# Start-up loads, a head-wise sum moved one step on, and a split output transfer in a two-block transformer kernel on one Trainium2 core

## The reference, cut to what matters

```python
def _rmsnorm(x, g, eps=EPS):
    xf = x.astype(jnp.float32)
    y = xf * lax.rsqrt(jnp.mean(xf * xf, axis=-1, keepdims=True) + eps)
    return (y * g.astype(jnp.float32)).astype(x.dtype)
...
    kk = heads(k * k_k)
    kk = kk / jnp.maximum(jnp.linalg.norm(kk, axis=-1, keepdims=True), 1e-12)
...
    bonus = jnp.sum(rh * kh * r_k.astype(jnp.float32), axis=-1, keepdims=True) * vh
    y = y + bonus.reshape(B, S, RW_WIDTH)
```

## Time and profile before

| | |
|---|---|
| median of three runs | 4110.72 us (4109.21 to 4110.77) |
| the profiled execution's own time | 4109.02 us |
| its span in the profile | 4107.2 us |
| granted TensorE clock, mean | 0.981 |
| TensorE matmul busy | 3915.6 us (95%) |
| VectorE, ScalarE, GpSimd busy | 1750.6, 604.4, 1216.3 us |
| weights read by SyncE's queue | 544.81 MB |

### The profile page before, as it was taken

How to read it: one execution, slowest core, us unless ns; L and a number is a source line. 1 busy time by engine, 2 the same in 40 slices (tenths; PEclk the granted TensorE clock), 3 DMA queues, 4 the chain that set the end, 5 groups by cost and what they waited for, 6 DMA issues and landing times.

```text
span 4107.2 us, 65406 instructions
## 1 busy us (share of the span) xinstructions
PE 3915.6 (95%) x28356; PEld 3601.6 (88%) x28356; DVE 1750.6 (43%) x3176; ACT 604.4 (15%) x1311; POOL 1216.3 (30%) x719
## 2 busy tenths in 40 slices
PE   8999999999999698999999999989998899999997
PEld 7788888888888698999999998877687899999997
DVE  1344425541111443111115447561432588887544
ACT  0333311111111101000000000131302111111001
POOL 0000000001110675777770000000151377775000
PEclk9999999999999898999999999999999999999998
DMA  6555654445543443444444554435332244444441
GB/s 237 188 202 200 219 208 172 168 163 219 191 166 116 152 147 120 165 165 168 176 168 153 170 200 166 160 106 176 66 136 103 105 165 167 175 173 160 164 161 71
DMA packets 105134, 665.69 MB, mean 162 GB/s; under 512 B 21712, under 2 KB 23840, under 8 KB 74384
## 3 DMA queue, kind: packets, MB, share of 16 engines
q1 hardware_dynamic: 61904, 544.81, 36.8%
q0 software_dynamic: 19408, 70.79, 5.4%
q10 hardware_dynamic: 23536, 45.92, 3.1%
HBM read 611.34 MB, written 50.13 MB: 161 GB/s over the span
## 4 chain that ended last, share of the span: by engine, by line
PE 92%; DVE 3%; ACT 2%; issue 1%; DVEq 1%; POOL 0%; ACTq 0%; DMA 0%; POOLq 0%
PE product_bank L538 47%; PE product_bank L586 31%; PE product_bank L382 3%; PE mixer_bank L1214 2%; PE mixer_bank L724 1%; PE mixer_bank L740 1%; PE mixer_bank L2149 1%; ACT xT L841 0%; PE mixer_bank L2150 0%; PE mixer_bank L1234 0%; DVE arena L1328 0%; PE mixer_bank L1104 0%; PE mixer_bank L2181 0%; PE mixer_bank L1086 0%; PE mixer_bank L2114 0%
## 5 line engine op out<-in xcount | busy, mean ns | idle before, releaser
L586 PE MATMUL product_bank<-hT,weight_ring 128*128 128x256 f32 x3648 | 815.6, 382 | 0.0
L586 PEld LDWEIGHTS product_bank<-hT,weight_ring 128*128 128x128 f32 x3648 | 693.9, 191 | 103.5 <-issue 8.3
L538 PE MATMUL product_bank<-hT,weight_ring 128*128 128x128 f32 x3680 | 457.5, 276 | 12.3 <-DVEq L1586 5.8
L538 PEld LDWEIGHTS product_bank<-hT,weight_ring 128*128 128x128 f32 x3680 | 435.9, 193 | 14.6 <-DVEq L1586 6.0
L538 PE MATMUL product_bank<-arena,weight_ring 128*128 128x128 f32 x3232 | 402.4, 275 | 0.0
L538 PEld LDWEIGHTS product_bank<-arena,weight_ring 128*128 128x128 f32 x3232 | 382.2, 192 | 0.6
L562 DVE TENSOR_TENSOR arena<-product_bank,arena 128x128 f32<-128x128 f32 x128 | 37.2, 291 | 744.9 <-PE product_bank L538 743.2
L505 POOL TENSOR_TENSOR arena<-weight_ring 128x1024 f32<-128x1024 f32 x90 | 212.3, 2359 | 420.0 <-PE product_bank L538 295.7
L2549 DVE SCALAR_TENSOR_TENSOR arena<-arena 128x256 f32<-128x256 f32 x176 | 321.9, 1867 | 14.7 <-ACT arena L2514 11.3
L508 POOL TENSOR_TENSOR weight_ring<-weight_ring 128x1024 f32<-128x1024 f32 x112 | 275.3, 2458 | 0.0
L538 PE MATMUL product_bank<-hT,arena 128*128 128x128 f32 x2048 | 250.2, 276 | 1.5 <-DVE hT L494 1.5
(11 more groups left out here) (490 smaller groups left out, 5395.0 us busy)
## 6 DMA issues: line engine op xcount, KB each, us to landing
weight_ring<-in_weights SPq DMA_DIRECT2D x213, 2048.0 KB, 8.1
weight_ring<-in_weights SPq DMA_DIRECT2D x128, 512.0 KB, 5.6
weight_ring<-in_weights SPq DMA_DIRECT2D x64, 384.0 KB, 5.6
units<-out_stage ACTq DMA_DIRECT2D x87, 256.0 KB, 7.9
rwkv_keep<-arena ACTq DMA_DIRECT2D x16, 1282.0 KB, 7.3
arena<-rwkv_keep POOLq DMA_DIRECT2D x8, 2048.0 KB, 9.4
arena<-units POOLq DMA_DIRECT2D x52, 256.0 KB, 3.8
arena<-units POOLq DMA_DIRECT2D x48, 128.0 KB, 6.0
```

Of the source, the lines that this page charges most:

```text
L538: mm = pe.matmul(bank[:, at * P:at * P + P], lhs[:, j, :], rhs[:, j, :], start=g == 0 and n in (0, 3) and j == 0, stop=g == n_groups - 1 a ...
L586: mm = pe.matmul(psg[b][:, half * T:half * T + T], lhs, rhs, start=k == 0, stop=k == 15)
```

## The change

The constants come in two transfers: columns 0 to 383 right behind x, under x's semaphore, which thereby counts to 32, and the rest behind the parameters. ScalarE, VectorE and TensorE wait for 32 at the start; TensorE waits for the rest of the constants only behind the first product stage. SyncE starts the weights once x, the first constants and the parameters are there, where before it waited for x and all constants. In step 2 of the first mixer the bonus sum moves behind the yield, so that the two quarters of products stand between the sum of kk squared and the bonus sum, which now stands at the head of step 3. The result is written in four transfers of 512 KB, each when its chunk of the last layer norm is done.

```diff
         def load_inputs(pool):
+            first = CONST_AT["ones_mean"][1]
             pool.dma_start(xT[:, :, :], t_in["xT"]).then_inc(sem("x_loaded"), 16)
-            pool.dma_start(consts[:, :], t_in["consts"]).then_inc(sem("consts_loaded"), 16)
+            pool.dma_start(consts[:, 0:first], t_in["consts"][:, 0:first]).then_inc(sem("x_loaded"), 16)
             pool.dma_start(params[:, :], t_in["params"]).then_inc(sem("params_loaded"), 16)
+            pool.dma_start(consts[:, first:], t_in["consts"][:, first:]).then_inc(sem("consts_loaded"), 16)
...
             for c, ck in enumerate(chunks_of):
-                act.wait_ge(sem(ready), count - NCK + 1 + c if ready != "x_loaded" else 16)
+                act.wait_ge(sem(ready), count - NCK + 1 + c if ready != "x_loaded" else 32)
...
                 pe.matmul(pm[0][:, 0:256], const("head_ones"), rw["sq"], start=True, stop=True)\
                     .then_inc(sem("rw1_kk_sum"), 1)
+                yield
                 pe.wait_ge(sem("rw1_norm"), b1)
                 pe.wait_ge(sem("rw1_cum"), b1)
                 pe.matmul(pm[0][:, 256:512], const("head_ones"), rw["rk"], start=True, stop=True)\
                     .then_inc(sem("rw1_bonus_sum"), 1)
-                yield
                 pe.wait_ge(sem("rw1_operands"), b1)
...
         def _(sp):
-            sp.wait_ge(sem("x_loaded"), 16)
-            sp.wait_ge(sem("consts_loaded"), 16)
+            sp.wait_ge(sem("x_loaded"), 32)
+            sp.wait_ge(sem("params_loaded"), 16)
             stream_weights(sp)
...
-            pool.wait_ge(sem("ln_done"), 3 * NCK)
-            pool.dma_start(t_out, xT[:, :, :]).then_inc(sem("out_written"), 16)
-            pool.wait_ge(sem("out_written"), 16)
+            for c, ck in enumerate(chunks_of):
+                pool.wait_ge(sem("ln_done"), 2 * NCK + c + 1)
+                pool.dma_start(t_out[:, ck, :], xT[:, ck, :]).then_inc(sem("out_written"), 16)
+            pool.wait_ge(sem("out_written"), 16 * NCK)
...
         def _(pe):
-            pe.wait_ge(sem("consts_loaded"), 16)
+            pe.wait_ge(sem("x_loaded"), 32)
             squares_pe(pe, "mix_pre", pm[0])
             products(pe, "lora", hT, ready="mix_in", count=NCK, chunks=NCK)
+            pe.wait_ge(sem("consts_loaded"), 16)
...
             dve.wait_ge(sem("params_loaded"), 16)
-            dve.wait_ge(sem("x_loaded"), 16)
+            dve.wait_ge(sem("x_loaded"), 32)
```

## The result

The changed kernel takes 4080.96 us (median of four runs, 4077.60 to 4081.02), the kernel before in the same session 4109.97 us (4108.53 to 4110.77): 29.0 us less, a ratio of 0.9929 (95% interval 0.9917 to 0.9941). 4079.7 had been forecast, 31.0 us less. Two later sessions gave 31.3 and 30.2 us less (4078.02 against 4109.27, 4079.30 against 4109.50). The profiled execution took 4077.6 us, its span is 4075.8 us; 31.4 us shorter than the span before.

The account below looks back on a forecast made before the run. TensorE was taken to bound the kernel, with 92% of the chain of waits. Gains of 27.4 (moved sum), 0.3 (start) and 3.3 (end) made 31.0 us, from 4110.7 to 4079.7, range 4072 to 4091.

Parts of the forecast that it names:

- What bounds it: Whole kernel: TensorE is 92% of the chain of waits; only closing its gaps or shortening the span's ends pays.
- The moved sum: First mixer, steps 2 and 3: waits for ScalarE's root go, 32.9 us removed, 5.5 given back, 27.4 net.
- The reasoning on the odd tile: First mixer, step 3: VectorE's operands come about 0.1 us late for TensorE, and the next wait swallows this.
- The end: Output: only 512 KB follow the last chunk, landing in 3.3 us instead of 6.6; 3.3 us gained.
- The start: TensorE's first sum of squares starts at 12.1 us instead of 12.44; 0.3 us gained.
- 192 KB by share is 0.46: Start: the first constants, 192 KB, were taken to delay ScalarE's table load by 0.46 us.
- Sum: Whole kernel: gains of 27.4, 0.3 and 3.3 add to 31.0 us, giving 4079.7 us.
- 3 us either way: Later waits: clock falls may move, 1.5 us each; two allowed either way, 3 us.
- the rival's 0.74 us: First mixer, step 3: VectorE's wait costs 0.74 us per tile, odd tiles more; about 4090 to 4094, chance 0.13.
- The inputs of even tiles: First mixer: inputs of every second tile come late and TensorE waits; slower, 4119 us, chance 0.03.

Follow-up runs that it names:

- the late copy: Kernel before, only ScalarE's copy of a finished unit one place later in its order: 4079.02 us against 4110.20.
- the start alone: Kernel before with only the changed start (constants in two parts, weights earlier): 4112.13 us against 4109.27.
- the output alone: Kernel before with only the result written in four transfers: 4105.63 us against 4109.27.

## Why the prediction was right, point by point

- **What bounds it** held: what was gained in the traces is a gap of TensorE closed, a record of TensorE at 2.4 instead of 1.2 GHz, or the end of the span.
- **The moved sum.** Forecast 32.9 removed, 5.5 given back, 27.4 net. The stage alone measured 28.4 by the trace, because 0.30 us came back per tile instead of 0.35, and a fall of the clock had cost up to 1.69 us instead of 1.54. (16 times 0.35 is 5.6, not 5.5; that slip is worth 0.1.) The reasoning on the odd tile, operands 0.1 us late and swallowed by the next wait, held: the gap is 0.30 on both kinds of tile. Why the odd wait was long (the copy ahead of the table load) was shown by the late copy, and also that ScalarE's order alone, with TensorE's left as it was, takes as much out of the whole.
- **The end.** Forecast 3.3, by a line between two transfers; measured 3.4 in the span, landings of 2.9. The estimate from the Trainium skill, "DMA: Bandwidth & Descriptors", "Anatomy of one DMA", had been 3.2 for the landing of 512 KB; 2.9 was measured. The Trainium skill's rule on the same page, "Rules for kernel authors", at least 1 MiB per DMA, is given there for bandwidth; here, where only the time to the last landing counted, the smaller transfers cost nothing that the trace shows.
- **The start** is the term that was mis-sized. "192 KB by share is 0.46" was half of the real delay of about 1.0 us behind x, so the sum began at 12.5 to 12.7 and not at 12.1. The forecast gain of 0.3 us became nothing. In the profile of the result the clock took another 1.1 us at the sum and 0.7 in the first products, and gave 1.4 back in the first tile, where the quarters that took 8.44 us before take 7.07.
- **Sum.** 31.0 forecast, 29.0 by the medians of the first session, 31.4 by the two profiled spans. The last two differ mostly because the profiled run was the shortest of its four; executions of one kernel are 4 to 6 us apart, where the prediction had allowed 3 us either way. That the total came so near is in part luck: the stage gave 1.0 us more than forecast and the start 0.3 less, and both are smaller than that spread.
- **Rivals.** VectorE's wait did move into step 3, at two fifths of the rival's 0.74 us, with nothing added on odd tiles. The inputs of even tiles: VectorE's shift (L940) waited for them, 1.8 us in two waits, TensorE never:

```profile
L940 DVE TENSOR_TENSOR arena<-arena 128x256 f32<-128x256 f32 x48 | 17.5, 421 | 45.4 <-ACT arena L1016 43.0 <-DMA arena<-units 1.8
```

Left open: whether the new start costs a microsecond or gives one, and why the clock falls behind one gap and not behind an equal one. It was not at random: in the profiles of the kernel before, of the start alone and of the output alone, the falls are behind the same four waits, the first, third, fifth and seventh of the eight long ones (155.59, 264.62, 373.74 and 482.91 us in the kernel before).

## What to carry to other kernels

Where TensorE waits for a chain over another engine, look first at what stands ahead of that chain on the other engine: a copy one place later took as much out as reordering TensorE did. A round trip from TensorE to another engine and back wants independent work of TensorE between its two ends: with the Gram products put there, the stage was 4.4 us shorter. And where an engine loads its table only when its data is there, as ScalarE did at the start, give it a small first use of that table ahead of the wait.

## What the runs showed of the hardware that was not expected

- A transfer of 192 KB issued right behind one of 2048 KB landed about 1.0 us behind it, while 145 KB issued behind 1280 KB of constants had landed 0.3 us behind those.
- The same 2.33 us gap of TensorE was followed by 1.2 GHz four times of eight, every second time, at 1.55 to 1.69 us each. Runs of one kernel differed by up to 6 us; two profiled ones, 4.5 us apart, had the same waits within 0.5 us each.
- ScalarE's table load of 1.28 us ran ahead of the wait of the root (L1044), but behind everything earlier in ScalarE's order. A copy that itself waits for the end of a unit held it back: that was the whole difference between a wait of 0.47 and one of 2.33 us. Not every load runs ahead: at the start (L712) it began when x had landed, at 9.35 us, and from the third tile on that of the sigmoid (L1035) began behind TensorE's L1075, where on the second tile it had run ahead. In the kernel's text the loads that ran ahead have one wait in front of their activation, these two have two; no run here tests whether that is the reason.
